# Query roots in the scale of the scores, a filled last differential head, and products between the last two norms

## The chip, the cores and the metric

The kernel runs on one NeuronCore of a Trainium2 chip. The metric is the device time of one execution in microseconds (us); lower is better. The engines named here are TensorE (PE, matrix products, its weight loads listed as PEld), VectorE (DVE), ScalarE (ACT), GpSimd (POOL) and SyncE (SP, which issues the loads).

## The reference

Two transformer blocks are computed one after the other on 512 tokens of 1024 features, in float32. The first has retention, differential attention over 8 heads, a convolution, a gated merge of the three, and a feed-forward part; then a norm. The second has a first SwiGLU part, neighbourhood attention (NA) and low-rank attention (MLA) side by side, their merge, and a second SwiGLU part. What the change touches is this:

```python
def _rmsnorm(x, g):
    y = x * lax.rsqrt(jnp.mean(x * x, axis=-1, keepdims=True) + RMS_EPS)
    return y * g

q = heads(_rmsnorm(cq, g_q) @ w_uq, N_HEADS_MLA)      # cq: 768 features of each token
s = jnp.einsum('bqhd,bkhd->bhqk', q * q.shape[-1] ** -0.5, k)
p = jax.nn.softmax(s, axis=-1)

attn = probs[:, :, 0] - lam * probs[:, :, 1]          # differential head, first block
merged = g0 * (ret @ w_branch[0]) + g1 * (diff @ w_branch[1]) + g2 * (conv @ w_branch[2])

x = x + gate * _rmsnorm(y, g_post)                    # residual of the MLA/NA merge
h = _rmsnorm(x, g_pre) * (1 + scale) + shift          # norm before the second SwiGLU
```

The root of a token's query is one factor for all 768 features of that token, and so for its whole row of scores.

## The kernel before

Activations lie with features on the partitions and tokens on the free axis, so a product takes a chunk of 128 output features by 512 tokens. Each float32 product is three products of parts rounded to fp32r: high by high, low by high, high by low. A chunk over 1024 input features is a **unit** of 24 matmuls (`unit`, L777, the matmuls at L791). Its weights pass through two buffers: SP loads `raw`, ACT copies the high part (`split`, L1444, `w_hi` at L1450), DVE subtracts for the low part (`split`, L2052, `w_lo` at L2056), and PE waits for the low part before the unit. SP may load a buffer again when the low part of the unit before is made; ACT may overwrite `w_hi` when the unit that used the buffer is done.

No scheduler orders the work. Each engine has its own program, written out in order, and semaphores tie them. Units are numbered, and the numbers fix the order of loads and splits: `U_BR` are the units of the branches' merge, `U_LORA` those of MLA's low-rank projections, `U_MLA` MLA's heads, `U_OUT2` the merged output, `U_FB` the second SwiGLU.

A head of attention leaves PE waiting for a softmax. So the kernel cuts units of the next head in parts and puts them (`fill`) between the steps of the present one. In `diff_head` (L934) the fill hangs on `more`, which is false in the last of the eight heads; that head's `qk`, `transpose_p` and `pv` steps stand alone, and `merge(1)` (L921) begins behind it with a gate unit (24 matmuls) and a branch unit.

Norms are of two kinds. A **norm over ones** (`sum_squares`, L798, the matmuls at L803) adds squares with a matrix of ones, then takes Ln and Exp on ACT (L1479, L1481), each of which loads its own function table. A **token norm** sums squares of each token into one column (`token_matmuls`, L809, 4 columns with two passes each, at L812), takes Sqrt on ACT (`token_root`, L1492), a reciprocal on DVE (`token_rooted`, L2101), and PE spreads the result over rows (`token_rows`, L830, at L775).

MLA's low-rank stage comes behind NA. PE turns NA's output (L775), runs the six `cq` units with a `sum_squares` for the keys among them, and `sum_squares` for the queries at their end. ACT copies each `cq` chunk out (L1926), splits the next weights and squares the chunk; DVE adds the squares (L2074). After the root DVE scales six chunks (L2752), ACT rounds them (`cq_hi`, L1502), DVE subtracts (`cq_lo`, L2115), and the first MLA unit takes them in turn. The unit of the rotated key part (`kr`, `U_LORA + 2`) was the fill of the last NA pair. Then the key and query parts are rotated (L1284 and L1289 on PE, L2742 to L2745 on DVE), and the first scores follow (L1324). Each score tile takes its maximum on DVE and Exp on ACT (L1957) with the constant scale 96^-0.5.

Between the merged output and the second SwiGLU stand two token norms: sums of the last chunks, root, rows, eight residual chunks on DVE (L2564, L2567), each squared on ACT (L1489) and summed on PE, then root, rows and the modulated input of the SwiGLU (L2560, L1713, L1502, L2115).

## Time and profile before

| | |
|---|---|
| three runs | 2969.21 us median (2966.67, 2969.56, 2969.21) |
| profiled execution | 2966.77 us, its span 2965.0 us |
| mean granted TensorE clock | 0.979 of full speed |
| PE busy | 2864.0 us (97% of the span) |
| DVE busy | 1486.9 us (50%) |
| ACT busy | 1163.1 us (39%) |
| DMA | 288.72 MB, mean 97 GB/s |

Times in the rows are counted from the start of the span. The granted clock is 1.00 at 2.4 GHz and 0.50 at 1.2 GHz. A busy PE can still be at the lower clock, or wait inside a group of matmuls, so the busy share alone doesn't say what a stage could give. Consecutive matmuls overlap in the rows: a pace is the distance between starts.

### The profile page before, as it was taken

What the parts mean: (1) busy time and instruction counts of PE and PEld (TensorE: products, weight loads), DVE (VectorE), ACT (ScalarE), POOL (GpSimd) and SP (SyncE); (2) the same over time, 40 slices, a digit from 0 to 9 for tenths busy, and PEclk for the clock granted to TensorE, in tenths of its full rate; (3) what the DMA queues carried; (4) which work ended last, traced back from release to release, by engine and by line L of the source; (5) the groups of instructions that cost most, each with busy time, mean ns of one, the idle gap of its engine ahead of it and who ended that gap; (6) DMA issues with size and microseconds to landing.
All of it is one profiled execution on the core that took longest, in us unless ns stands there. A gap on an engine that the chain in (4) does not pass through costs nothing.

```text
span 2965.0 us, 42739 instructions
## 1 busy us (share of the span) xinstructions
PE 2864.0 (97%) x14922; PEld 2362.3 (80%) x14922; DVE 1486.9 (50%) x2321; ACT 1163.1 (39%) x1791; POOL 34.0 (1%) x28
## 2 busy tenths in 40 slices
PE   8999999899999999999999999989989999899998
PEld 6778888679987888879998888877767778688887
DVE  3325455455565666567654473553344444433334
ACT  4323465432223322246633232355545443432223
POOL 0000000000000000000000000000000000000000
PEclk9999999899999999999999999999989999899999
DMA  3224211243343545536653333331111123133332
GB/s 114 70 65 134 79 51 56 64 139 110 119 140 103 154 144 157 163 107 193 178 142 93 92 94 97 87 84 50 49 29 48 34 54 99 54 92 93 92 92 85
DMA packets 504092, 288.72 MB, mean 97 GB/s; under 512 B 17577, under 2 KB 483962, under 8 KB 503850
## 3 DMA queue, kind: packets, MB, share of 16 engines
q1 hardware_dynamic: 503978, 287.25, 33.1%
q8 instruction: 66, 1.08, 0.2%
q14 instruction: 48, 0.39, 0.0%
HBM read 285.12 MB, written 2.10 MB: 97 GB/s over the span
## 4 chain that ended last, share of the span: by engine, by line
PE 73%; issue 19%; DVE 3%; ACT 3%; DVEq 1%; ACTq 0%; DMA 0%; POOL 0%; POOLq 0%; SPq 0%
PE unit_acc L791 65%; PE aux L775 2%; PE aux L1324 1%; PE unit_acc L1348 1%; PE unit_acc L1225 1%; DVE w_lo L2056 1%; ACT w_hi L1450 1%; PE aux L812 1%; PE aux L918 1%; PE aux L1206 1%; ACT h_hi L1502 0%; PE aux L1289 0%; ACT w_hi L1734 0%; DVE tmp L2405 0%; ACT L1496 0%
## 5 line engine op out<-in xcount | busy, mean ns | idle before, releaser
L791 PE MATMUL unit_acc<-h_hi,w_hi 128*128 128x512 f32 (+1 forms) x2376 | 829.3, 373 | 18.2 <-DVE h_lo L2115 9.4
L791 PE MATMUL unit_acc<-h_hi,w_lo 128*128 128x512 f32 (+1 forms) x2376 | 810.2, 365 | 0.0
L791 PE MATMUL unit_acc<-h_lo,w_hi 128*128 128x512 f32 (+1 forms) x2376 | 810.1, 365 | 0.0
L2056 DVE TENSOR_TENSOR w_lo<-raw,w_hi 128x1024 fp32r<-128x1024 f32 (+3 forms) x418 | 495.4, 1185 | 510.0 <-ACT w_hi L1450 503.3
L1450 ACT ACTIVATE w_hi<-raw 128x1024 fp32r<-128x1024 f32 (+3 forms) x418 | 430.5, 1030 | 699.2 <-PE unit_acc L791 655.5
L791 PEld LDWEIGHTS unit_acc<-h_hi,w_hi 128*128 128x128 f32 x2376 | 427.5, 190 | 111.7 <-issue 14.9
L791 PEld LDWEIGHTS unit_acc<-h_hi,w_lo 128*128 128x128 f32 x2376 | 426.6, 189 | 76.4
L791 PEld LDWEIGHTS unit_acc<-h_lo,w_hi 128*128 128x128 f32 x2376 | 428.1, 190 | 71.0
L791 PE MATMUL unit_acc<-branch_hi,w_hi 128*128 128x512 f32 x448 | 178.2, 398 | 0.0
L791 PE MATMUL unit_acc<-branch_hi,w_lo 128*128 128x512 f32 x448 | 177.6, 397 | 0.0
L791 PE MATMUL unit_acc<-branch_lo,w_hi 128*128 128x512 f32 x448 | 177.6, 396 | 0.0
L2229 DVE SCALAR_TENSOR_TENSOR ada_sum<-ada_raw,silu_c,ada_sum 128x512 f32<-128x512 f32 x203 | 145.8, 749 | 17.6 <-issue 12.2
L791 PE MATMUL unit_acc<-u_hi,w_hi 128*128 128x512 f32 x352 | 140.3, 398 | 0.0
L791 PE MATMUL unit_acc<-u_hi,w_lo 128*128 128x512 f32 x352 | 139.5, 396 | 0.0
L791 PE MATMUL unit_acc<-u_lo,w_hi 128*128 128x512 f32 x352 | 139.5, 396 | 0.0
L791 PE MATMUL unit_acc<-ctx_h_hi,w_hi 128*128 128x256 f32 (+1 forms) x440 | 129.0, 293 | 4.0 <-DVE w_lo L2056 2.1
L791 PE MATMUL unit_acc<-ctx_h_lo,w_hi 128*128 128x256 f32 (+1 forms) x440 | 127.0, 289 | 0.0
L791 PE MATMUL unit_acc<-ctx_h_hi,w_lo 128*128 128x256 f32 (+1 forms) x440 | 126.8, 288 | 0.0
L791 PEld LDWEIGHTS unit_acc<-branch_hi,w_lo 128*128 128x128 f32 x448 | 84.3, 188 | 20.5
L791 PEld LDWEIGHTS unit_acc<-branch_hi,w_hi 128*128 128x128 f32 x448 | 84.4, 188 | 20.4 <-DVE w_lo L2056 0.2
L791 PEld LDWEIGHTS unit_acc<-branch_lo,w_hi 128*128 128x128 f32 x448 | 84.5, 189 | 20.2
L2498 DVE TENSOR_TENSOR w_lo<-raw,w_hi 128x1024 fp32r<-128x1024 f32 (+1 forms) x66 | 78.5, 1191 | 42.9 <-ACT w_hi L1734 42.9
(367 smaller groups left out, 3610.3 us busy)
## 6 DMA issues: line engine op xcount, KB each, us to landing
raw<-in_ffn_w_dram SPq DMA_DIRECT2D x180, 512.0 KB, 3.9
raw<-in_w_in_dram SPq DMA_DIRECT2D x142, 512.0 KB, 3.9
ada_raw<-in_w_ada_dram SPq DMA_DIRECT2D x72, 512.0 KB, 4.7
raw<-in_w_up_dram SPq DMA_DIRECT2D x32, 512.0 KB, 4.2
raw<-in_w_down_dram SPq DMA_DIRECT2D x32, 512.0 KB, 3.9
raw<-in_w_branch_dram SPq DMA_DIRECT2D x24, 512.0 KB, 4.0
raw<-in_ffn_w_dram SPq DMA_DIRECT2D x24, 384.0 KB, 3.4
raw<-in_w_out_dram SPq DMA_DIRECT2D x16, 512.0 KB, 3.9
```

Of the source, the lines that this page charges most:

```text
L775: return pe.transpose(dst, src, ident[k0:k0 + k, k0:k0 + k])
L791: last = pe.matmul(G[s][0:n, 512 * j:512 * j + m], w[:, k, 0:n], x[:, k, a:a + m], start=(k == 0 and i == 0), stop=(k == kc - 1 and i == 2))
L812: done = pe.matmul(dst[:, t:t + 1], src[:, P * t:P * t + P], ones[:, 0:1], start=(first and t == 0), stop=(last and t == NT - 1))
L918: last = pe.matmul(A[1][:, a:a + 1], s[:, c * P:c * P + P], ones[:, 0:1], start=True, stop=True)
L1206: last = pe.matmul(A[0][:, 512 * e + b:512 * e + b + 256], nq[r, P * t:P * t + P], k[r, k0:k0 + 256], start=True, stop=True)
L1225: last = pe.matmul(NA_OUT[:, 64 * e:64 * e + 64], nT[:, e, j, :], nV[:, v, 64 * e:64 * e + 64], start=(e == 0 and j == 0), stop=(e == 1 an ...
L1324: last = pe.matmul(A[0][:, a:a + m], mq[0:QK, P * t:P * t + P], mk[0:QK, a:a + m], start=True, stop=True)
L1348: last = pe.matmul(MLA_OUT, mT[t % 2][:, j, :], mV[:, j, :], start=(j == 0), stop=(j == 5))
L1450: act.activation(wh[v.slot][:, 0:kc, :], raw[v.slot][:, 0:kc, :], ACT.Copy).then_inc(hi_split, 1)
L2056: dve.tensor_tensor(wl[s][:, 0:kc, :], raw[s][:, 0:kc, :], wh[s][:, 0:kc, :].bitcast(F32), ALU.subtract).then_inc(lo_split, 1)
L2229: last = dve.scalar_tensor_tensor(out=s[:, :], in0=w, scalar=c, in1=s[:, :], op0=ALU.mult, op1=ALU.add)
L2498: dve.tensor_tensor(wl[s][:, 0:kc, :], raw[s][:, 0:kc, :], wh[s][:, 0:kc, :].bitcast(F32), ALU.subtract).then_inc(lo_split, 1)
```

## The change

Five things are changed.

1. **Last differential head.** `diff_head` with `more` false takes the gate unit `U_BR[1]` in parts (`gate`): 6 matmuls behind `qk(4)`, 6 behind `qk(2)`, 3 behind `qk(1)`, 6 behind `pv(1)`, 3 behind the turn of the output. `merge(1, 1)` leaves that unit out.
2. **Root tables.** `root_table` takes a Sqrt of a constant ahead of the squares at the first block's output and at the tail of both SwiGLUs and of the second block's output. At three roots DVE's split of weights and the reciprocal change places, or ACT's.
3. **MLA query norm.** `cq` is no longer scaled. ACT squares it from PSUM and makes `cq_hi` with the gain, DVE makes `cq_lo` and adds the squares (`cq_step`, `cq_low`), token sums replace the second `sum_squares`, and the root goes, per query row, into `qsc`, which the maximum and Exp of each score tile use as scale. The `kr` unit moves from `U_LORA + 2` behind the `cq` units, so `cq` unit 0 is now the last fill of NA, and SP's loads move with it. NA's turns stand two ahead of unit 1 and two ahead of unit 2.
4. **Rotation of the key part** moves behind the first MLA unit and into the other auxiliary PSUM tile.
5. **Products between the last two norms.** `turn_over` issues 3, 4, 8, eight times 2, and 8 matmuls of 128x512 whose result nobody reads.

```diff
@@ PE
+            def merge(r, gated=0):
                 for h in range(2):
...
+                        for k in range(4):
+                            merge_pair(r, Count(U_BR[r] + 2 * k), k >= gated)
...
+                def gate(k0, k1):
+                    if not more:
+                        unit(Count(U_BR[1]), HH, HL, GM, part=(k0, k1))
...
-            pe.wait_ge(n_o, 16 + 1)
-            for c in range(4):
...
-            unit(Count(U_LORA + 3), H2H, H2L, GS)
+            pe.wait_ge(n_o, 16 + 1)
+            for half in range(2):
+                for c in range(2):
+                    na_rows(2 * half + c)
+                unit(Count(U_LORA + 3 + half), H2H, H2L, GS)
             pe.wait_ge(n_lo, 4)
             sum_squares(ss2, G2)
-            for k in range(1, 6):
-                unit(Count(U_LORA + 3 + k), H2H, H2L, GS)
-            pe.wait_ge(k_kr, 1)
-            pe.matmul(A[1][0:QK, 0:SEQ], cst("rot", 0, QK), mkr[0:QK, CTX:T2], start=True, stop=True).then_inc(k_rot, 1)
-            sum_squares(ss2, GS)
+            for k in range(3, 6):
+                unit(Count(U_LORA + 2 + k), H2H, H2L, GS)
+            unit(Count(U_LORA + 8), H2H, H2L, GS, n=QK, part=(0, 5))
+            token_sums_added(cqa, cqs, TOK[1], 6)
+            unit(Count(U_LORA + 8), H2H, H2L, GS, n=QK, part=(5, 8))
...
-            unit(Count(U_MLA), CQH, CQL, GS, kc=6, n=QK, ready=(ap_lo, 6 * KC + 2))
+            unit(Count(U_MLA), CQH, CQL, GS, kc=6, n=QK, ready=(q_lo, 0))
+            pe.wait_ge(k_kr, 1)
+            pe.matmul(A[0][0:QK, 0:SEQ], cst("rot", 0, QK), mkr[0:QK, CTX:T2], start=True, stop=True).then_inc(k_rot, 1)
...
+                for _ in range(n):
+                    pe.matmul(G[0][:, 512:1024], MH2[:, 0, 0:P], MH2[:, 0, :], start=True, stop=True)
+
+            turn_over(3)
             token_sums_added(ss2, tm2)
+            turn_over(4)
             token_rows(0)
+            turn_over(8)
             for c in range(KC):
                 token_sums(c, tm2)
+                turn_over(2)
             token_rows(1)
-            swiglu(U_FB, 6 * KC + 8, 76)
+            turn_over(8)
+            swiglu(U_FB, 6 * KC + 2, 76)
@@ ACT
+            def root_table():
+
+                act.activation(tok_std[:, NT:NT + 1], eps_col, ACT.Sqrt)
...
+                token_square(k, acc(G[v.slot], GS), cqs, SEQ)
+                act.activation(CQH[:, k, :], acc(G[v.slot], GS), ACT.Copy, scale=col_b[:, 64 + k:65 + k]).then_inc(q_hi, 1)
+                split(v + 2)
...
-                    act.activation(mP[b][:, :], A[0][:, 0:T2], ACT.Exp, bias=mst[:, b, 1:2], scale=QK ** -0.5,
+                    act.activation(mP[b][:, :], A[0][:, 0:T2], ACT.Exp, bias=mst[:, b, 1:2], scale=qsc[:, 0, t:t + 1],
@@ DVE
+                dve.scalar_tensor_tensor(out=CQL[:, k, :], in0=acc(G[s], GS), scalar=col_b[:, 64 + k:65 + k],
+                                         in1=CQH[:, k, :].bitcast(F32), op0=ALU.mult,
+                                         op1=ALU.subtract).then_inc(q_lo, 1)
+                dve.drain().then_inc(evicted[s], 1)
+                token_add(cqa[:, :], cqs, k, 6)
```

The pieces of each engine's order that the prediction rests on follow. On PE in the last differential head, from its first scores (`qk(4)`, 512 and 16 columns) on, before:

```order
L954 MATMUL aux<-diff_k_102,diff_q_100 128x512 x2
L959 MATMUL aux<-diff_k_102,diff_q_100 128x16 x2
L954 MATMUL aux<-diff_k_102,diff_q_100 128x400 x2
L775 MATMUL aux<-const,diff_vT 128x128 x4
L775 MATMUL aux<-const,diff_vT 16x128
L775 MATMUL aux<-const,diff_p_105 128x128 x4
L775 MATMUL aux<-const,diff_p_105 16x128
L954 MATMUL aux<-diff_k_102,diff_q_100 128x272 x2
L981 MATMUL aux<-diff_v,diff_pT_109 128x128 x5
```

and from `qk(2)` (272 columns) on, after:

```order
L968 MATMUL aux<-diff_k_102,diff_q_100 128x272 x2
L794 MATMUL unit_acc<-h_hi,w_hi_51 128x512
L794 MATMUL unit_acc<-h_lo,w_hi_51 128x512
L794 MATMUL unit_acc<-h_hi,w_lo_53 128x512
L794 MATMUL unit_acc<-h_hi,w_hi_51 128x512
L794 MATMUL unit_acc<-h_lo,w_hi_51 128x512
L794 MATMUL unit_acc<-h_hi,w_lo_53 128x512
L995 MATMUL aux<-diff_v,diff_pT_109 128x128 x5
```

Six matmuls of the gate unit now stand between `qk(2)` and the `pv` step that followed it at once; `gate(0, 2)` stands in the same way behind the 16-column row.

On ACT at the end of MLA's query stage, before:

```order
L1926 ACTIVATE cq<-unit_acc 128x512
L1450 ACTIVATE w_hi_52<-raw_50 128x1024
L1462 ACTIVATE tmp_1_155<-cq 128x512
L1479 ACT_TABLE_LOAD
L1479 ACTIVATE rstd_157<-aux,const 128x512
L1481 ACT_TABLE_LOAD
L1481 ACTIVATE rstd_157<-rstd_157 128x512
L1502 ACTIVATE cq_hi<-tmp_0_154 128x512
L1502 ACTIVATE cq_hi<-tmp_1_155 128x512
```

and after:

```order
L1527 ACTIVATE cq_sq_200<-unit_acc 128x512
L1912 ACTIVATE cq_hi<-unit_acc,col_b 128x512
L1488 ACTIVATE w_hi_51<-raw_49 128x1024
L1986 ACT_TABLE_LOAD
L1986 ACTIVATE tok_std<-unit_acc,const 128x4
L1989 ACTIVATE mla_kr<-unit_acc 96x512
L1488 ACTIVATE w_hi_52<-raw_50 128x1024
L1996 ACTIVATE mla_q_213<-unit_acc 96x512
```

Both roots over 512 columns and the rounding of six scaled chunks are gone; a root of 4 columns stands between the splits.

On PE between the last two norms (`ssq` and `tmp` are the sums of squares, `tok_rstd` the rows), before:

```order
L791 MATMUL unit_acc<-merged_hi,w_lo_54 128x512
L812 MATMUL aux<-const,ssq_156 128x1 x4
L812 MATMUL aux<-const,tmp_1_155 128x1 x4
L775 MATMUL aux<-const,tok_rstd 128x128 x4
L812 MATMUL aux<-const,tmp_0_154 128x1 x4
L812 MATMUL aux<-const,tmp_1_155 128x1 x4
```

and after:

```order
L1453 MATMUL unit_acc<-merged_hi 128x512 x3
L815 MATMUL aux<-const,ssq_156 128x1 x4
L815 MATMUL aux<-const,tmp_1_155 128x1 x4
L1453 MATMUL unit_acc<-merged_hi 128x512 x4
L778 MATMUL aux<-const,tok_rstd 128x128 x4
L1453 MATMUL unit_acc<-merged_hi 128x512 x8
L815 MATMUL aux<-const,tmp_0_154 128x1 x4
L1453 MATMUL unit_acc<-merged_hi 128x512 x2
L815 MATMUL aux<-const,tmp_1_155 128x1 x4
L1453 MATMUL unit_acc<-merged_hi 128x512 x2
```

The unread matmuls (L1453) stand between every two steps, the sums of each residual chunk included.

## Rows read from the trace of the kernel before

**Rows 1.** The page: busy time, share of the span and instructions of each engine.

```profile
PE 2864.0 (97%) x14922; PEld 2362.3 (80%) x14922; DVE 1486.9 (50%) x2321; ACT 1163.1 (39%) x1791; POOL 34.0 (1%) x28
```

**Rows 2.** Windows of the low-rank stage: length, PE, PEld, DVE, ACT, POOL, granted clock, DMA.

```profile
2119.04:2189.66 70.62, 52.07 (x208) 37.25 (x206) 34.97 (x46) 37.68 (x48) 0.00 (x0) 0.90 0.19 52
2125.04:2129.73 4.69, 4.69 (x22) 3.76 (x20) 2.10 (x3) 2.92 (x3) 0.00 (x0) 1.00 0.13 38
2142.40:2144.96 2.56, 2.56 (x7) 2.00 (x6) 1.18 (x2) 0.00 (x0) 0.00 (x0) 0.50 0.72 200
```

**Rows 3.** PE's timeline in the last head: start, length, instruction, [idle before <-releaser].

```profile
544.07 1.53 PE L954 MATMUL aux<-diff_k,diff_q 64*128 64x400 f32 x4 [2.68 <-DVE diff_nb L2306]
...
549.23 1.30 PE L775 MATMUL aux<-const,diff_p 128*128 128x128 f32 x5 [2.37 <-DVE diff_p L2322]
...
568.07 1.12 PE L775 MATMUL aux<-const,diff_on 128*128 128x128 f32 x4 [2.64 <-DVE diff_on L2339]
```

**Rows 4.** Busy time by stretch: the last head's slow part, and the gate unit behind it.

```profile
544.40:571.60 27.20, 20.41 (x70) 13.41 (x67) 11.76 (x37) 10.46 (x39) 1.01 (x1) 0.50 0.13 39
568.84:575.75 6.91, 6.91 (x26) 5.53 (x25) 3.05 (x5) 0.69 (x1) 0.00 (x0) 0.80 0.01 2
```

**Rows 5.** DVE's timeline at the end of that head.

```profile
569.94 0.75 DVE L2345 SCALAR_TENSOR_TENSOR branch_lo<-aux,small,branch_hi 128x512 fp32r<-128x512 f32 x1 [1.93 <-ACT branch_hi L1638]
```

**Rows 6.** Busy time by stretch: the residual chunks, and three stretches for the clock.

```profile
2547.66:2559.14 11.48, 9.25 (x44) 9.25 (x44) 10.88 (x16) 4.25 (x7) 0.00 (x0) 0.50 0.14 41
1943.76:1947.17 3.41, 1.33 (x11) 1.33 (x12) 2.96 (x4) 3.13 (x5) 0.00 (x0) 1.00 0.08 16
1947.17:1950.60 3.43, 3.43 (x18) 3.43 (x18) 2.87 (x4) 2.05 (x4) 0.00 (x0) 0.50 0.63 168
2572.90:2579.00 6.10, 3.85 (x13) 1.94 (x13) 4.77 (x7) 4.92 (x8) 0.00 (x0) 1.00 0.00 0
```

**Rows 7.** The root's table loads in the whole trace: count, ns min/median/max, first and last.

```profile
L1496 ACT ACT_TABLE_LOAD  x4: 1283/1283/1283, 951.5 to 2952.4; - x4
```

**Rows 8.** DVE's timeline, the last weight split and one scaled chunk.

```profile
2166.51 1.23 DVE L2056 TENSOR_TENSOR w_lo<-raw,w_hi 128x1024 fp32r<-128x1024 f32 x1 [3.60 <-ACT w_hi L1450]
...
2175.87 0.68 DVE L2115 TENSOR_TENSOR cq_lo<-tmp,cq_hi 128x512 fp32r<-128x512 f32 x1
```

**Rows 9.** PE's timeline in the low-rank stage, its waits.

```profile
2123.01 1.25 PE L775 MATMUL aux<-const,na_o 128*128 128x128 f32 x8 [2.94 <-DVE na_oT_lo L2722]
...
2140.36 0.50 PE L791 MATMUL unit_acc<-h_hi,w_hi 128*128 128x512 f32 x1 [3.57 <-DVE w_lo L2056]
...
2168.58 1.66 PE L803 MATMUL aux<-ssq,const 128*128 128x512 f32 x2 [3.06 <-DVE ssq L2074]
2175.26 0.71 PE L791 MATMUL unit_acc<-cq_hi,w_hi 128*96 128x512 f32 x1 [5.02 <-DVE cq_lo L2115]
...
2184.64 1.02 PE L1289 MATMUL aux<-mla_q,const 96*96 96x512 f32 x2
...
2189.66 2.07 PE L1324 MATMUL aux<-mla_k,mla_q 96*128 96x512 f32 x2 [2.50 <-DVE mla_q L2745]
```

**Rows 10.** PE's timeline between the last two norms.

```profile
2542.99 1.05 PE L812 MATMUL aux<-const,tmp 128*128 128x1 f32 x8
2546.51 1.11 PE L775 MATMUL aux<-const,tok_rstd 128*128 128x128 f32 x4 [2.46 <-DVE tok_rstd L2106]
2549.89 13.81 PE L812 MATMUL aux<-const,tmp 128*128 128x1 f32 x64 [2.27 <-ACT tmp L1489]
...
2568.52 0.77 PE L791 MATMUL unit_acc<-h_hi,w_hi 128*128 128x512 f32 x1 [3.14 <-DVE h_lo L2115]
```

**Rows 11.** ACT's timeline, the last but one query chunk.

```profile
2159.07 0.60 ACT L1926 ACTIVATE cq<-unit_acc 128x512 f32<-128x512 f32 x1 [3.11 <-PE unit_acc L791]
2159.81 1.06 ACT L1450 ACTIVATE w_hi<-raw 128x1024 fp32r<-128x1024 f32 x1
```

**Rows 12.** The Exp of MLA's 32 score tiles in the whole trace.

```profile
L1957 ACT ACTIVATE mla_p<-aux,mla_stat x32: 901/902/903, 2193.8 to 2415.1; 128x768 f32<-128x768 f32 x32
```

More of the change, by code:

```diff
@@ L401, in build @@
         CKL = at("ckv_lo", o, [2, T2], F32R); o += 8 * T2
-        cqT = at("cq", o, [6, SEQ]); o += 6 * 2048
+        cqs = [at(f"cq_sq{s}", o + s * 2048, [SEQ]) for s in range(2)]
+        cqa = at("cq_sum", o + 4096, [SEQ]); o += 6 * 2048
         CQ = o
@@ L989, in diff_head @@
                 fill(0, 0, 4)
+                gate(0, 2)
                 qk(3)
@@ L1000, in diff_head @@
                 fill(1, 0, 3)
+                gate(2, 4)
                 pv(4)
@@ L1004, in diff_head @@
                 fill(1, 3, 6)
+                gate(4, 5)
                 pv(3)
@@ L1012, in diff_head @@
                 fill(2, 2, 6)
+                gate(5, 7)
                 pe.wait_ge(d_on, val(turn(i, 1 + e, 2)))
@@ L1017, in diff_head @@
                 fill(2, 6, 8)
+                gate(7, 8)
             for k in range(3):
@@ L1187, in fill @@
                 def fill(k, k0, k1):
-                    unit(u + 3 + k, H2H, H2L, GS, n=QK if k == 2 and last_pair else P, part=(k0, k1))
+                    unit(u + 3 + k, H2H, H2L, GS, part=(k0, k1))
                 def token_v(half):
@@ L1908, in _, with na_high @@
                     na_pair(i, p, (i, p) == (1, 1))
-            for c in range(4):
+            def na_high(c):
                 act.wait_ge(n_ot, c + 1)
@@ L2723, in _ @@
                                   ALU.subtract).then_inc(n_lo, 1)
+            cq_low(0)
+            split(Count(U_LORA + 4))
+            for c in range(2):
+                na_low(c)
             for k in range(2):
                 add_square(ss2[:, :], tm2, T2, k == 0)
-            rooted()
-            scaled(2, lambda c: tm2[c % 2][:, :], lambda c: CKH[:, c, :], lambda c: CKL[:, c, :],
-                   lambda c, b: dve.scalar_tensor_tensor(out=b, in0=ckvT[:, c, :], scalar=col_b[:, 70 + c:71 + c],
-                                                         in1=rs2[:, :], op0=ALU.mult, op1=ALU.mult))
@@ L2732, in _ @@
-            for k in range(6):
-                split(Count(U_LORA + 5 + k))
-                add_square(ss2[:, 0:SEQ], tm2, SEQ, k == 0)
+            split(Count(U_LORA + 5))
+            for c in range(2, 4):
+                na_low(c)
+            cq_low(1)
+            cq_low(2)
+            split(Count(U_LORA + 6))
+            rooted()
+            for c in range(2):
+                dve.scalar_tensor_tensor(out=tm2[c][:, :], in0=ckvT[:, c, :], scalar=col_b[:, 70 + c:71 + c],
+                                         in1=rs2[:, :], op0=ALU.mult, op1=ALU.mult).then_inc(ap_tmp, 1)
@@ new lines, in _ @@
+            cq_low(3)
+            split(Count(U_LORA + 7))
+            for c in range(2):
+                nap[0] += 1
+                dve.wait_ge(ap_hi, nap[0])
+                dve.tensor_tensor(CKL[:, c, :], tm2[c][:, :], CKH[:, c, :].bitcast(F32), ALU.subtract).then_inc(ap_lo, 1)
+            for k in range(4, 6):
+                cq_low(k)
+                split(Count(U_LORA + 4 + k))
+            dve.drain()
+            dve.wait_ge(q_root, 1)
+            dve.reciprocal(tok_rstd[:, 0:NT], tok_std[:, 0:NT])
```

134 lines of the change are left out of this document (79 added, 55 removed).

## Prediction

> **What bounds the kernel now.** I read the page first: PE is busy for 97% of the span, DVE for 50%, ACT for 39% [rows 1]. So the kernel is bound by TensorE, and a change of order can give back only two things: the idle time of PE, and the stretches in which its granted clock is 0.50. I then read PE's timeline for its waits, and the windows for the clock. A matmul of 512 columns takes 4.69 / 20 = 0.2345 us warm and 2.56 / 6 = 0.427 us cold (the counts of PEld give the 20 and the 6) [rows 2]. A unit of 24 is 5.63 us warm, 10.2 cold. The reader should see that every place touched has both losses, and that they hang together: a wait is followed by a slow stretch.
>
> All sums below are against the profiled execution: 2966.8 us, a span of 2965.0 and 1.8 around it. The median of the three runs is 2.4 above that.
>
> **Last differential head.** The head waits 2.68 us for its second mask, 2.37 for its first probabilities and 2.64 for the normalised output [rows 3], and it runs at clock 0.50 from 544.4 to 571.6, with PE busy for 20.4 of 27.2 us [rows 4]. Then the gate unit takes 6.91 us, partly cold [rows 4]. The edit lays that unit's 24 matmuls into the head: 6 in the first wait, 6 ahead of `pv(4)`, 3 and 6 further on, 3 at the end. What is late next is the branch unit, which needs `branch_lo`, made at 570.69 [rows 5], against its start at 575.75, where the gate unit ends [rows 4]. With an unchanged head the gain is 575.75 - 570.69 = 5.1. The gate parts delay the head where PE was not waiting: 6 matmuls ahead of `pv(4)`, 1.4 us warm and 2.6 cold, partly taken back in later waits. Against that the head itself gets faster where the clock holds: 20.4 us busy at 0.50 would be 10.2 at full speed, though DVE and ACT own a part of the chain, so I count 6 to 7 of it. Warm throughout: 5.1 + 6.3 + nothing lost = 11.4. Cold throughout: 5.1 less 2.6 less some 1.5 for a branch unit that starts cold = 1. In the first wait 1.4 of 2.68 us is filled and the fall at 544.4 should go, but the second wait keeps 2.37 us and has no fill (the fill comes behind it). A comparable stretch, 1.33 us busy of 3.41 [rows 6], was followed by one at 0.50. So I expect one slow stretch of about 7 us around `pv(4)`, at a price of 3.4 (half its length): **-8**, bounds -1 and -11.4.
>
> **Roots with their table loaded ahead.** Four root table loads of 1.283 us are in the trace [rows 7]. The last of them, at 2952.4, stands at the kernel's end, where all that follows is on the path; it begins some way into the last sums of squares, so I count two thirds of it: **-0.9**, bounds 0 and -1.3. Behind the first SwiGLU the whole load is in the way of the rows, but DVE's split of weights (1.23 us [rows 8]), which lay beside it, now stands between root and residual. PE gets its rows and its next unit 1.2 earlier, the residual chunks start as before: **-1.2**, bounds +0.5 (if the residual sets the pace) and -2.5. At the first block's output the sums cover most of the load: **-0.25**. At the last but one norm the same exchange of split and root holds the residual where it is; its load was hidden by nothing, but see below.
>
> **MLA's query stage.** From 2119.04 to the first scores at 2189.66 are 70.6 us with PE busy for 52.1 [rows 2]. I build the new one from the same durations. NA's turns, first two: 1.04; the unit behind them, 5.63, covers the wait of 2.94 for `na_oT_lo` [rows 9]; turns 1.0; unit 5.63, which covers the making of NA's low parts; sums for the keys 1.0; three units 16.9; `kr` 5.6, cut at 5/8 by the token sums, two groups of 8 at about the 1.05 us of the row before the last norms [rows 10], 1.9; first MLA unit, 18 matmuls, 4.2 (from its start at 2175.26 to the query's rotation at 2184.64 are 9.4 [rows 9], less the second unit's 2.1 it took 7.3, since `cq_lo` came chunk by chunk; that and the 5.02 ahead of it go); rotation of the key, two wide matmuls (1.66 for such a pair while it waited [rows 9]), 1.0; second MLA unit, 12 matmuls of 384 columns, 12 x 0.2345 x 0.75 = 2.1. To here 46.0, so 2165.1 less what overlaps. Then the first scores need the rotated query. Before, from the query's rotation on PE to the scores were 5.0 us with a wait of 2.50 [rows 9]. Beside this PE chain stands a chain of DVE: rotation of the key on PE ends near 2163, then three DVE steps at the 0.68 of a 512-column step [rows 8], 2.1, two copies 1.1, two splits of 768 and 256 columns (1.23 is for 1024 [rows 8]) 1.4, three steps for the query 2.1: 2170.0. Both chains end at 2169.8 to 2170.1. **-19.8**.
>
> What can go less well: the wait of 3.57 for `w_lo` [rows 9] came when DVE and ACT had the keys' root between the splits. That work still stands there, and each `cq` round is now longer: on ACT a square and a copy from PSUM (0.60 each [rows 11]) ahead of the 1.06 of `w_hi` [rows 11]; on DVE `cq_lo` and the sum (0.7 each) ahead of the 1.23 of `w_lo` [rows 8]. With hand-overs this is 4.3 us from the end of a unit to the weights of the next but one, against 5.63 that PE has for the unit between. The tight round is `cq` unit 5, 0.2 us to spare by my sum. If that wait comes back at its old 3.57 and brings its cold stretch of 3.4 us (price 1.7), the gain is 19.8 - 5.3 = 14.5; I keep 13 as the low bound and 21 as the high one (the 0.50 stretch avoided and the key's rotation earlier).
>
> **Scales by pointer.** Exp has 768 columns in 0.902 us with one pointer operand [rows 12]; copies have 0.60 for 512 and 1.06 for 1024 [rows 11], so 0.83 for 768. A pointer then costs up to 0.07, 32 times: 2.3 at most if all of it is on the path, nothing at the least, since PE's fills lie beside most tiles. I take **+0.5**. On DVE the maximum's scale is in the same case.
>
> **Products between the last two norms.** Before, PE waits 2.46 for the rows, 2.27 for the first square, then runs 64 one-column matmuls in 13.81 us (1.73 per chunk), at clock 0.50 [rows 6, 10]. DVE's eight chunks take 11.48 us, 1.44 each [rows 6]: less than PE's 1.73. So this stretch is set by a cold PE. The residual starts no earlier: the 3 + 4 products and the moved split (1.23) take what the hidden table load gives. Then each chunk costs PE its 8 sums and 2 products. If the clock stays at 0.50: 1.73 + 2 x 0.427 = 2.58 per chunk, 0.85 more; over the seven chunks ahead of the last sums 6.0, and 0.3 more since the last pair delays the rows: **+6.3**. If it holds at 1.00: 8 sums at 0.95 or so and 0.47, about DVE's 1.44, so DVE sets the pace: 8 x (1.73 - 1.44) = 2.3 and a little at the rows, -2.6. The 8 products behind the rows fall in the wait of 3.14 for `h_lo` [rows 10] and cost nothing warm, 0.3 cold. Which it is I read from the windows. The sums alone kept PE busy for 9.25 of 11.48 us and the clock was 0.50 [rows 6]: busy by one-column matmuls does not raise it. With the products, full-width work is 0.47 of 1.44 us, a third. 1.33 of 3.41 (39%) was followed by 0.50, 3.85 of 6.10 (63%) stayed at 1.00 [rows 6]. A third lies on the side of the fall. The page "TensorE: Matmul & The Clock Gate" of the Trainium skill, section "HAM oscillation — how this bites in real kernels", gives as the abstract rule that PE must have no long idle gaps, and by it the clock would hold, since the longest gap left is under 1.5 us. The rows speak against it here, as the stretch of sums had small gaps too and stayed slow; the rule's outcome is the first rival.
>
> Sum: 2966.8 - 8 - 0.9 - 1.2 - 0.25 - 19.8 + 0.5 + 6.3 = 2943.4; on the median of the shown runs 2945.8. Forecast **2945**, its own range 2939 to 2951.
>
> **Rivals.**
> - *The clock holds between the last norms.* The products fill every gap, and 8 of them stand ahead of the first sums. For it: the stretch begins warm behind a full unit. Against it: the shares above. Its term is -2.6 in place of +6.3: 2936.
> - *The head stays cold, or the `cq` rounds slip.* For it: the wait of 2.37 is unfilled and 6 cold matmuls then delay `pv(4)`; the margin of 0.2 at `cq` unit 5. Against it: full-width matmuls in four places of the head. With -1 for the head 2952; with 13 for MLA's stage 2952 as well; both 2959.
> - *Slower: PE waits in every `cq` round.* ACT reads each chunk twice from PSUM and DVE once, ahead of the next split. If the round takes longer than 5.63, PE waits seven times, and if each wait is followed by the low clock, as that of 3.57 was, all seven units run at 10.2: 7 x 4.6 = 32 us more than planned, 2945 + 32 = 2977. It decides from a round of some 6.5 us on, 2.2 more than my 4.3; against it also that a cold unit gives the others time, so that the next wait would go.
> - *It does nothing*, the gains of MLA's stage being eaten by the tail behind it: against it, the six scaled chunks are on the path as their own five waits show, and they are gone.
>
> **How the numbers follow.** Forecast 0.62, clock holds 0.20, cold head or slipped rounds 0.14, slower 0.03, nothing 0.01. The range runs from 2933 (the first rival with the head warm) to 2956 (the second, short of both together). A measurement of this kernel can tell about 0.2%, 5.9 us, from no change. The first three cases lie all but wholly below 2963: faster 0.95; same 0.02; slower 0.03.
>
> **What would show it.** In the changed kernel's profile: the last head with a branch unit starting 8 us nearer to `qk(4)` and one slow stretch; the first MLA scores some 50.8 us behind NA's last fill, no wait over 1 us in the six units, no wait ahead of the first MLA unit; the token sums between the last norms at 2.6 us per chunk and clock 0.50 (1.4 and 1.00 would be the rival); the Exp at 0.90 to 1.0 us. The forecast is wrong if the stretch between the last norms is shorter than before, if the head is still cold throughout, or if the `cq` units wait for `w_lo`.

## The result, and the profile after

The changed kernel takes 2945.55 us (median of four runs, 2942.68 to 2947.37) against 2967.94 before (four runs, 2961.93 to 2969.56), a ratio of 0.9927 with a 95% interval of 0.991 to 0.9945. Faster, by 22 us; 2945 was predicted. The profiled execution took 2945.81 with a span of 2944.0, against 2966.77 and 2965.0. The page of after (busy time and instructions; the chain that ended last, which on the page before was PE 73%, issue 19%):

```profile
PE 2866.4 (97%) x14975; PEld 2368.9 (80%) x14975; DVE 1482.9 (50%) x2317; ACT 1159.8 (39%) x1787; POOL 33.9 (1%) x28
...
PE 82%; issue 8%; DVE 5%; ACT 3%; DVEq 1%; ACTq 0%; DMA 0%; POOL 0%; POOLq 0%; SPq 0%
```

PE is as busy as before. The chain's shares say little about the gain: "issue", time in which an engine waited for nothing that the profile shows, fell by 11 points of the span, some 330 us by the two pages, for a gain of 21. So the reading goes by stretches. Since all marks of the program can be found in both traces, the 21.0 us of difference between the spans can be laid out by stretch. Each row is the distance between the starts of two instructions on PE (the last: on DVE):

| stretch | before | after | difference | predicted |
|---|---|---|---|---|
| start to `qk(4)` of the last head | 540.13 | 540.95 | +0.8 | 0 |
| to the first branch unit behind it | 35.62 | 28.38 | -7.2 | -8 |
| to the rows of the first block's norm | 377.59 | 377.31 | -0.3 | -0.25 |
| to the sums at the first SwiGLU's tail | 953.55 | 953.66 | +0.1 | 0 |
| to the rows there | 3.66 | 2.41 | -1.25 | -1.2 |
| to the first unit on the latent tokens | 48.92 | 50.42 | +1.5 | 0 |
| to NA's turns | 159.57 | 159.52 | 0 | 0 |
| to MLA's first scores | 70.62 | 50.67 | -19.95 | -19.8 |
| to MLA's turns (eight heads) | 233.98 | 234.78 | +0.8 | +0.5 |
| to the end of the last output unit | 118.50 | 118.37 | -0.1 | 0 |
| to the turn of x, behind the first unit of the second SwiGLU | 43.28 | 48.87 | +5.6 | +6.3 |
| to the sums at the end | 365.01 | 364.99 | 0 | 0 |
| to the output on DVE | 3.87 | 3.04 | -0.8 | -0.9 |

**The last head.** PE's timeline, the rows that answer to [rows 3], and the branch unit:

```profile
544.88 0.94 PE L968 MATMUL aux<-diff_k,diff_q 64*128 64x400 f32 x4 [1.08 <-DVE diff_nb L2366]
...
549.45 1.30 PE L778 MATMUL aux<-const,diff_p 128*128 128x128 f32 x5 [2.93 <-DVE diff_p L2382]
...
554.61 1.62 PE L995 MATMUL aux<-diff_v,diff_pT 128*128 128x128 f32 x10
...
569.33 0.39 PE L794 MATMUL unit_acc<-branch_hi,w_hi 128*128 128x512 f32 x1
```

The first wait is 1.08 us instead of 2.68, the third is gone, the second has grown from 2.37 to 2.93. `pv(4)` starts at 554.61, 5.2 behind the turn of the probabilities (2.4 before). The clock in that stretch, and in a fast one and a slow one behind it:

```profile
549.45:554.61 5.16, 5.16 (x15) 3.46 (x16) 3.04 (x10) 1.87 (x6) 0.00 (x0) 0.50 0.54 165
555.00:561.00 6.00, 4.79 (x32) 3.45 (x30) 2.81 (x13) 3.15 (x14) 0.00 (x0) 1.00 0.03 13
562.00:568.00 6.00, 5.49 (x15) 3.43 (x15) 0.86 (x2) 1.50 (x8) 1.01 (x1) 0.50 0.01 3
```

So the head has two slow stretches, 548.1 to 554.9 and 561.8 to 568.6, instead of one of 27 us.

**The low-rank stage.** Its window, and PE's rows that answer to [rows 9]:

```profile
2112.65:2163.32 50.67, 47.23 (x221) 36.66 (x219) 30.11 (x42) 30.81 (x40) 0.00 (x0) 0.99 0.23 64
```

```profile
2151.16 0.39 PE L794 MATMUL unit_acc<-cq_hi,w_hi 128*96 128x512 f32 x1
...
2155.35 1.02 PE L1424 MATMUL aux<-mla_kr,const 96*96 96x512 f32 x2
...
2163.32 2.08 PE L1348 MATMUL aux<-mla_k,mla_q 96*128 96x512 f32 x2 [2.50 <-DVE mla_q L2838]
```

PE waits for 3.4 of 50.7 us, all of it behind the second MLA unit, and the clock is 1.00 up to there. None of the waits of 2.94, 3.57, 3.06 and 5.02 us is left.

**Between the last two norms.** PE and then DVE, the rows that answer to [rows 10]:

```profile
2519.88 0.60 PE L778 MATMUL aux<-const,tok_rstd 128*128 128x128 f32 x4
...
2523.97 1.48 PE L815 MATMUL aux<-const,tmp 128*128 128x1 f32 x8 [1.64 <-ACT tmp L1527]
2525.31 1.20 PE L1453 MATMUL unit_acc<-merged_hi 128*128 128x512 f32 x2
2526.31 1.70 PE L815 MATMUL aux<-const,tmp 128*128 128x1 f32 x8
2527.87 1.20 PE L1453 MATMUL unit_acc<-merged_hi 128*128 128x512 f32 x2
...
2544.23 1.05 PE L778 MATMUL aux<-const,tok_rstd 128*128 128x128 f32 x4
```

```profile
2520.60 1.23 DVE L2116 TENSOR_TENSOR w_lo<-raw,w_hi 128x1024 fp32r<-128x1024 f32 x1 [1.08 <-ACT w_hi L1488]
2521.75 0.74 DVE L2624 SCALAR_TENSOR_TENSOR y<-y,res_gain,aux 128x512 f32<-128x512 f32 x1
```

The rows are there at 2519.88, but DVE first waits for `w_hi`, splits, and starts the residual at 2521.75; PE then waits 1.64 us for the first square. During the first chunk the clock falls, and from then on each chunk costs 2.56 us: eight sums at 1.56 and two products together at 1.00 (2526.31, 2527.87). DVE's residual was done by 2533.2, eleven us before PE.

**The root at the first SwiGLU's tail.** DVE before and after, and the ACT Exp of all MLA tiles, which answers to [rows 12]:

```profile
1908.69 1.23 DVE L2056 TENSOR_TENSOR w_lo<-raw,w_hi 128x1024 fp32r<-128x1024 f32 x1 [2.04 <-ACT w_hi L1450]
1910.32 0.18 DVE L2106 RECIPROCAL tok_rstd<-tok_std 128x4 f32<-128x4 f32 x1 [0.40 <-ACT tok_std L1496]
1911.71 0.75 DVE L2564 SCALAR_TENSOR_TENSOR y<-y,res_gain,aux 128x512 f32<-128x512 f32 x1 [1.21 <-PE aux L775]
```

```profile
1902.47 0.18 DVE L2166 RECIPROCAL tok_rstd<-tok_std 128x4 f32<-128x4 f32 x1 [2.44 <-ACT tok_std L1538]
1904.20 1.22 DVE L2116 TENSOR_TENSOR w_lo<-raw,w_hi 128x1024 fp32r<-128x1024 f32 x1 [1.55 <-ACT w_hi L1488]
1905.35 0.74 DVE L2624 SCALAR_TENSOR_TENSOR y<-y,res_gain,aux 128x512 f32<-128x512 f32 x1
```

```profile
L2015 ACT ACTIVATE mla_p<-aux,mla_stat,mla_scale x32: 991/992/994, 2167.6 to 2389.6; 128x768 f32<-128x768 f32 x32
```

From the sums (1906.89 before, 1900.30 after) the reciprocal comes at 3.43 before and 2.17 after, the residual at 4.82 and 5.05: the split now stands between.

### The profile page after: what moved, and what is told of

It reads as the page before. It is cut to its first block, busy times and chain, and to the rows that moved or that the text cites. A ratio compares the mean times of both kernels' runs of the same rounds, so it can differ in the third digit from the quotient of the medians.

```text
span 2944.0 us, 42823 instructions
## 1 busy us (share of the span) xinstructions
PE 2866.4 (97%) x14975; PEld 2368.9 (80%) x14975; DVE 1482.9 (50%) x2317; ACT 1159.8 (39%) x1787; POOL 33.9 (1%) x28
## 4 chain that ended last, share of the span: by engine, by line
PE 82%; issue 8%; DVE 5%; ACT 3%; DVEq 1%; ACTq 0%; DMA 0%; POOL 0%; POOLq 0%; SPq 0%
PE unit_acc L794 71%; PE aux L778 3%; PE unit_acc L1372 1%; PE aux L1348 1%; DVE w_lo L2116 1%; PE aux L995 1%; PE unit_acc L1244 1%; PE aux L968 1%; ACT w_hi L1488 1%; PE aux L815 1%; PE aux L921 1%; PE aux L1225 1%; DVE diff_p L2356 0%; PE unit_acc L1453 0%; ACT mla_p L2015 0%
```

## The experiments

Small differences are read in their own stretch of the trace, because the same instructions elsewhere vary by more (last section). These are the stretches on which the readings rest, in us, from the profiled execution of each:

```
                     qk(4) to   SwiGLU 1   rows to   NA turns    MLA's     last output
                     branch     sums to    first     to first    eight     unit to
                     unit       rows       unit      scores      heads     turn of x
before               35.62      3.66       48.92     70.62       233.98    43.28
after                28.38      2.41       50.42     50.67       234.78    48.87
e1_no_turn           28.69      2.41       50.62     50.67       233.51    42.52
e2_mla_only          34.46      3.67       48.14     50.67       233.56    43.28
e3_turn_only         35.64      3.67       50.82     71.69       234.03    44.73
e4_head_only         28.40      3.66       49.06     70.43       232.55    43.29
e5_head_wait         27.69      2.41       51.95     50.67       233.53    47.95
e6_late_split        28.48      2.41       50.31     50.67       234.81    43.88
e7_turn_six          28.58      2.41       51.97     50.67       234.94    48.04
e8_combined          27.71      2.41       50.45     50.67       234.81    40.93
e9_turn_eight        27.69      2.41       51.72     50.67       233.57    40.53
e10_rotate_first     27.23      2.41       51.95     49.08       233.75    40.91
e11_const_scale      28.59      2.41       50.42     50.67       233.51    48.02
e12_turns_together   28.42      2.41       51.85     56.88       233.49    46.37
```

### One part of the change at a time

e1_no_turn takes the unread products out of the changed kernel:

```diff
-            turn_over(3)
             token_sums_added(ss2, tm2)
-            turn_over(4)
             token_rows(0)
-            turn_over(8)
             for c in range(KC):
                 token_sums(c, tm2)
-                turn_over(2)
             token_rows(1)
-            turn_over(8)
```

> The changed kernel without the 39 unread products between the last two norms. Theory (the products lengthen a stretch that stays at clock 0.50): 5.6 us less than the changed kernel, about 2940, ratio to the kernel before 0.9905; token sums back at 1.73 us per chunk, clock 0.50 there. Rival (the products pay for themselves, by keeping the clock up in front of the second SwiGLU): the same time as the changed kernel or more, 2945 to 2949.

Measured: 2940.34 us (2936.42 to 2942.94), ratio 0.9909 (0.9894 to 0.9925). The stretch is 42.52 instead of 48.87, 6.35 less. The products cost a little more than was said (5.6); the rival falls. The median moved by 5.2; in the profiled execution other stretches, of the same instructions, happened to be longer by 3.1, 1.5 and 1.1.

e2_mla_only is the changed kernel with all but the MLA part taken back:

```diff
-                    if not more:
+                    if False:
                         unit(Count(U_BR[1]), HH, HL, GM, part=(k0, k1))
-            merge(1, 1)
+            merge(1)
-            root_table()
-            turn_over(3)
...
```

> The kernel before with the new query norm of MLA alone (with the moved key unit, the moved turns of NA and the scales by pointer); no gate unit in the last head, no root tables, no unread products. Theory (terms are independent): 19.9 less in the low-rank stage and 0.7 more for the scales, 19.3 less in all, ratio 0.9935. Rival (a part of the 20 us comes from the phase in which the stage starts, and would be smaller without the filled head): 10 to 15 less, ratio 0.995 to 0.9965.

Measured: 2945.86 (2943.4 to 2948.13), ratio 0.993 (0.9917 to 0.9944), 20 us. The low-rank stage is 50.67, to the hundredth that of the changed kernel. The gain doesn't depend on where the stage begins.

e3_turn_only adds the products alone to the kernel before:

```diff
+            turn_over(3)
             token_sums_added(ss2, tm2)
+            turn_over(4)
             token_rows(0)
+            turn_over(8)
             for c in range(KC):
                 token_sums(c, tm2)
+                turn_over(2)
             token_rows(1)
+            turn_over(8)
```

> The kernel before with the 39 unread products alone. The table load (1.28 us) is not hidden here, so the gaps are wider. Theory: slower by 5.5 to 6.5 us, ratio 1.002, clock 0.50 in the sums. Rival (the products hold the clock at 1.00 in this place): faster by 2 to 3 us, ratio 0.999.

Measured: 2967.68 (2963.83 to 2971.54, eleven runs), ratio 1.0007 (0.9998 to 1.0016). Neither number came: the stretch is 1.45 us longer than before, not 5.5. PE's timeline of this kernel:

```profile
2548.54 0.65 PE L775 MATMUL aux<-const,tok_rstd 128*128 128x128 f32 x4 [0.80 <-DVE tok_rstd L2116]
...
2551.45 1.05 PE L812 MATMUL aux<-const,tmp 128*128 128x1 f32 x8 [0.41 <-ACT tmp L1499]
...
2552.92 1.01 PE L812 MATMUL aux<-const,tmp 128*128 128x1 f32 x8
...
2557.55 1.70 PE L812 MATMUL aux<-const,tmp 128*128 128x1 f32 x8
```

Here the wait ahead of the first sums is 0.41 us. The first three chunks run at clock 1.00, 1.43 to 1.46 us each, the fourth takes 1.77; only then comes the slow pace of 2.56. In this kernel DVE's split still lies ahead of the reciprocal, so the residual starts 0.7 behind the rows, not 1.9.

e4_head_only adds the gate unit's parts alone:

```diff
+                gate(0, 2)
...
+                gate(2, 4)
                 pv(4)
...
-            merge(1)
+            merge(1, 1)
```

> The kernel before with the gate unit laid into the last differential head alone. Theory: the branch unit starts 28.4 us behind qk(4) instead of 35.6, 7.2 less in all, ratio 0.9976. Rival (the gain is given back by the merge behind it, whose weights come later): under 3 less, ratio 0.999 to 1.

Measured: 2956.36 (2950.96 to 2957.31), ratio 0.9964 (0.995 to 0.9977). The stretch is 28.40, and the merge behind it is as long as before (377.57 to the norm's rows, 377.59 before): nothing is given back. The median is 9.4 below that of before, more than the 7.2 of the stretch; the rest is not traced to anything.

### Why the products didn't hold the clock

e6_late_split moves DVE's split of weights behind the residual chunks; the products stay:

```diff
             token_rooted()
-            split(Count(U_OUT2 + 1 + KC))
             residual(1, ROW[0])
+            split(Count(U_OUT2 + 1 + KC))
```

> The changed kernel with DVE's split of weights between the last two norms moved behind the eight residual chunks; the unread products stay. It shortens the wait of 1.64 us ahead of the first sums to about 0.4. From the end of the last output unit to the turn of x: 43.28 us before the change, 48.87 after it, 44.73 with the products alone on the kernel before. Theory (the longer wait lets the clock fall at the first chunk instead of the fifth): 43 to 44, five to six us less than the changed kernel, the first four chunks at 1.4 us and clock 1.00. Rival (the share of full-width work alone decides, the wait does not): the start comes 1.25 earlier and all chunks stay at 2.6, 47.6.

Measured: 2942.88 (2936.25 to 2943.93), ratio 0.9922 (0.9909 to 0.9936); the stretch is 43.88, in the theory's range. PE's timeline:

```profile
2522.68 1.05 PE L815 MATMUL aux<-const,tmp 128*128 128x1 f32 x8 [0.41 <-ACT tmp L1527]
...
2524.14 1.02 PE L815 MATMUL aux<-const,tmp 128*128 128x1 f32 x8
...
2528.93 1.70 PE L815 MATMUL aux<-const,tmp 128*128 128x1 f32 x8
```

With a wait of 0.41 instead of 1.64 us the clock is 1.00 for three chunks (1.46, 1.43 and 1.42 us) and a part of the fourth (1.95), then it falls as well. In the changed kernel it falls in the first.

That the wait makes this difference is not shown. e5_head_wait, e11_const_scale and e12_turns_together below have the same instructions in this stretch as the changed kernel, and the same wait of 1.64, but the stretch takes 47.95, 48.02 and 46.37 us instead of 48.87. In the first two the slow pace comes with the second chunk, in e12_turns_together with the third:

```profile
2528.64 1.05 PE L815 MATMUL aux<-const,tmp 128*128 128x1 f32 x8 [1.64 <-ACT tmp L1527]
...
2530.11 1.02 PE L815 MATMUL aux<-const,tmp 128*128 128x1 f32 x8
...
2531.54 1.21 PE L815 MATMUL aux<-const,tmp 128*128 128x1 f32 x8
```

So behind one and the same wait the fall comes 0.5 to 3.6 us behind the start of the first sums (four traces); with a wait of 0.41 it comes 5.1 and 5.3 us behind it (e6_late_split, e3_turn_only). That speaks for the theory. But counted from the end of the last output unit the clock falls at 11.1 us in e12_turns_together and at 11.4 in e6_late_split, nearly at the same time with either wait. One trace of each doesn't part the wait from the scatter. What the earlier split gives for certain is the earlier start of the sums, 1.2 to 1.3 us.

e7_turn_six has six products behind each chunk:

```diff
                 token_sums(c, tm2)
-                turn_over(2)
+                turn_over(6)
```

> The changed kernel with six unread products behind each chunk's sums instead of two. Theory (more full-width work holds the clock, 1.41 of 2.4 us): clock 1.00 through all eight chunks at 2.4 us each, 19 us for them, about what they take with two (20.5). Rival (the clock is low in this place whatever PE does): 1.73 + 2.56 = 4.3 us a chunk, 14 us slower.

Measured: 48.04 for the stretch, where the changed kernel has 48.87, and clock 1.00 from the second chunk on:

```profile
2521.71 1.27 PE L815 MATMUL aux<-const,tmp 128*128 128x1 f32 x8 [1.62 <-ACT tmp L1527]
2522.84 2.91 PE L1453 MATMUL unit_acc<-merged_hi 128*128 128x512 f32 x6
...
2527.95 0.95 PE L815 MATMUL aux<-const,tmp 128*128 128x1 f32 x8
2528.76 1.65 PE L1453 MATMUL unit_acc<-merged_hi 128*128 128x512 f32 x6
```

```profile
2528.80:2541.61 12.81, 12.81 (x78) 11.22 (x79) 2.22 (x4) 2.80 (x5) 3.52 (x1) 1.00 0.00 0
```

The clock in this place follows what PE does. But a chunk takes 2.3 us (the first 3.8, since its six products ran slow), more than 1.73 at the low clock without products: holding the clock costs more than it gives, when the work that it speeds up are one-column sums.

### Where the head's time is

e5_head_wait puts nine of the gate unit's matmuls where PE waits longest:

```diff
+                gate(2, 5)
                 transpose_p(4)
                 qk(2)
-                gate(2, 4)
                 pv(4)
                 transpose_p(3)
                 qk(1)
-                gate(4, 5)
```

> The changed kernel with nine of the gate unit's matmuls laid into the wait for the first probabilities (2.93 us, empty so far), in place of the six behind qk(2) and the three behind qk(1). Theory (that empty wait makes the clock fall for 6.7 us, and the six matmuls delay the first pv): clock 1.00 from qk(4) to pv(4), the branch unit 25 us behind qk(4) instead of 28.4, 3.4 us less in all than the changed kernel. Rival (the softmax chain of DVE and ACT sets the head's length): 27.5 to 28.4, under 1 us less.

Measured: 2946.61 (2944.49 to 2946.84), ratio 0.9937 (0.9924 to 0.9951). The head is 27.69, 0.7 shorter, in the rival's range. Its timeline and its clock:

```profile
544.26 0.50 PE L794 MATMUL unit_acc<-h_hi,w_hi 128*128 128x512 f32 x1 [0.83 <-ACT diff_v L1661]
...
546.46 0.71 PE L778 MATMUL aux<-const,diff_p 128*128 128x128 f32 x5
...
548.00 1.57 PE L995 MATMUL aux<-diff_v,diff_pT 128*128 128x128 f32 x10 [0.17 <-ACT diff_pT L1644]
550.90 0.66 PE L778 MATMUL aux<-const,diff_p 128*128 128x128 f32 x4 [1.33 <-DVE diff_p L2381]
```

```profile
541.79:552.28 10.49, 7.87 (x45) 5.17 (x45) 6.53 (x20) 6.64 (x21) 0.00 (x0) 1.00 0.30 100
552.28:565.55 13.27, 11.98 (x36) 8.40 (x37) 4.09 (x16) 4.15 (x18) 1.01 (x1) 0.51 0.01 1
```

The first slow stretch is gone, as the theory said, and `pv(4)` starts 10.1 behind `qk(4)` instead of 13.7. But PE then waits 1.33 us for the next probabilities, and the second slow stretch begins at once and lasts to the end of the head: 13 us instead of 6.8. Of 3.5 us won, 2.8 went there.

### Versions that might beat both

e8_combined is e1_no_turn with the edits of e5_head_wait and e6_late_split.

> The changed kernel without the unread products, with the nine gate matmuls in the empty wait of the last head and with DVE's split behind the residual chunks. Theory: 5.6 + 0.8 less from the products (as in the run without them), 3.4 from the head, 1.25 from the split: ratio to the kernel before 0.989, about 2934. Rival (a gain ahead of a stage is given back by the clock in the next): no better than the run without products alone, 0.991.

Measured: 2939.41 (2935.15 to 2942.32), ratio 0.9917 (0.9903 to 0.993). In its stretches: 27.71 for the head, and 40.93 between the norms, 1.59 less than e1_no_turn (1.25 was expected). As a whole it fell short of what was expected, and its interval overlaps that of e1_no_turn, so the times alone don't tell them apart.

e9_turn_eight puts eight products back behind the first rows of e8_combined:

```diff
             token_rows(0)
+            turn_over(8)
             for c in range(KC):
                 token_sums(c, tm2)
```

> The combined kernel with eight unread products put back in one place only, behind the first rows, where PE waits 2.27 us for the first square. From the end of the last output unit to the turn of x it is 40.93 us in the combined kernel. Theory (a filled wait lets the clock fall later, as with the late split, and nothing is added between the sums): the first two or three chunks at 1.43 instead of 1.73, 40.0 to 40.3. Rival (eight products only move the fall by their own length, the sums start later behind them): 40.9 to 41.5.

Measured: 2938.24 (2935.17 to 2940.76), ratio 0.9913 (0.9896 to 0.9929); the stretch 40.53. Between the two. PE shows why:

```profile
2518.70 1.12 PE L778 MATMUL aux<-const,tok_rstd 128*128 128x128 f32 x4 [0.57 <-DVE tok_rstd L2161]
2519.47 3.22 PE L1452 MATMUL unit_acc<-merged_hi 128*128 128x512 f32 x8
2522.53 2.04 PE L815 MATMUL aux<-const,tmp 128*128 128x1 f32 x16
2524.94 10.12 PE L815 MATMUL aux<-const,tmp 128*128 128x1 f32 x48 [0.37 <-ACT tmp L1522]
```

The clock had already fallen while PE waited 0.57 for the rows (1.12 us for them instead of 0.65), the products ran slow (3.22 us for eight), and the clock came back to 1.00 for two chunks and into the third.

e10_rotate_first, on e8_combined, changes two places:

```diff
+            mla_ready(0, 0, 0)
             for k in range(2):
                 split(Count(U_MLA + 2 + k), 2 if k else 6)
-            mla_ready(0, 0, 0)
...
-                gate(2, 5)
+                gate(2, 4)
                 transpose_p(4)
                 qk(2)
                 pv(4)
+                gate(4, 5)
                 transpose_p(3)
```

> The combined kernel with two changes that are read in their own stretches. (1) DVE rotates the first query ahead of the two splits of weights. Theory (the chain rotation of the key, copies, splits, rotation of the query is what the first scores wait for): from NA's turns to the first scores 49.1 instead of 50.67. Rival (PE's own chain is as long, as the prediction's sum had it): 50.3 to 50.7. (2) In the last head the gate unit's three matmuls that stood in the wait for the first probabilities stand behind the first pv, in a wait of 1.33: theory (a low clock behind the first pv sets the rest) 26.5 to 27 us from qk(4) to the branch unit instead of 27.7; rival (chain of DVE and ACT) 27.7. Together about 2 us less than the combined kernel if both theories hold.

Measured: 2935.32 (2932.94 to 2935.54), ratio 0.99 (0.9883 to 0.9916), the lowest median of the study, though its interval overlaps those of e8 and e9. From NA's turns to the first scores it takes 49.08:

```profile
2158.60 1.02 PE L1313 MATMUL aux<-mla_q,const 96*96 96x512 f32 x2
...
2162.03 1.56 PE L1348 MATMUL aux<-mla_k,mla_q 96*128 96x512 f32 x4 [0.91 <-DVE mla_q L2833]
```

The wait ahead of the scores is 0.91 instead of 2.50: the DVE chain was the end of that stage, 1.6 us behind PE's own. The head is 27.23, between theory and rival.

### Two sizes inside MLA

e11_const_scale leaves the query's root out of the scores:

```diff
-                    act.activation(mP[b][:, :], A[0][:, 0:T2], ACT.Exp, bias=mst[:, b, 1:2], scale=qsc[:, 0, t:t + 1],
+                    act.activation(mP[b][:, :], A[0][:, 0:T2], ACT.Exp, bias=mst[:, b, 1:2], scale=QK ** -0.5,
...
-                    dve.tensor_scalar(mst[:, b, 1:2], mst[:, b, 0:1], qsc[:, 1, t:t + 1], None, ALU.mult).then_inc(k_log, 1)
+                    dve.tensor_scalar(mst[:, b, 1:2], mst[:, b, 0:1], -(QK ** -0.5), None, ALU.mult).then_inc(k_log, 1)
```

> The changed kernel with the constant scale back in the Exp and the maximum of MLA's score tiles; the query's root is left out of the scores. From the first scores to MLA's turns it is 234.78 us in the changed kernel and 233.98 before. Theory (the pointer costs 0.09 us per tile and is on the path in some tiles): 234.0 to 234.3. Rival (the difference is the clock's, 0.2 to 0.8 in such a stretch from run to run): no different from 234.8 beyond that.

Measured: 233.51 for the eight heads, a little below what the theory gave. It decides little, since the ten kernels with the pointer have 233.49 to 234.94 (mean 234.1) and the four without 232.55 to 234.03 (mean 233.5). The Exp takes 902 ns here and 992 with the pointer, 32 x 0.09 = 2.9 in all. The means differ by 0.6, which is within the scatter, so no share of the 2.9 is shown to be on the path.

e12_turns_together undoes one detail of the order:

```diff
-            for half in range(2):
-                for c in range(2):
-                    na_rows(2 * half + c)
-                unit(Count(U_LORA + 3 + half), H2H, H2L, GS)
+            for c in range(4):
+                na_rows(c)
+            for half in range(2):
+                unit(Count(U_LORA + 3 + half), H2H, H2L, GS)
```

> The changed kernel with the four turns of NA's output together again, ahead of query unit 1, instead of two ahead of unit 1 and two ahead of unit 2. From NA's turns to the first scores it is 50.67 us in the changed kernel and 70.62 before. Theory (the unit between the turns hides the making of NA's low parts, a wait of 2.9 us before): 53.5 to 54, with a wait of about 3 for na_oT_lo. Rival (the rounds of DVE and ACT behind it take the wait up, since PE then asks later for each weight): 51 to 52.

Measured: 56.88, 6.2 more than the changed kernel, twice what the theory gave. PE, and then a window over most of the unit behind:

```profile
2117.20 1.97 PE L778 MATMUL aux<-const,na_o 128*128 128x128 f32 x8 [3.53 <-DVE na_oT_lo L2793]
```

```profile
2118.83:2125.60 6.77, 6.77 (x24) 5.42 (x23) 0.62 (x1) 0.00 (x0) 0.00 (x0) 0.72 0.16 47
```

The wait is 3.53. Nearly all of the other 2.7, which the theory left out, are matmuls at the low clock behind it: the last two turns take 0.8 more than in the changed kernel, and the two units behind them 1.6 more. This is a single run, but the stretch takes 50.67 in all nine traces that have the changed kernel's instructions there. So some 6 of the 20 us of this stage come from two turns put elsewhere.

## Why the prediction was right, point by point

**The head, -8 forecast, -7.2 measured** (e4_head_only alone: -7.2). The step was to expect the first wait filled, the second empty, and one slow stretch of 7 us around `pv(4)`. That stretch is there, 548.1 to 554.9, just ahead of `pv(4)`. A second one of 6.8 us at the end was not foreseen. Priced like the first, at half its length, it would cost 3.4, but the forecast missed by only 0.8; so another part of the head's sum was too cautious by some 2.6 (an estimate from these two numbers), and that the number came so close is in part luck. That the rest of the head's length is DVE's and ACT's was put in as "6 to 7 of 10.2", and e5_head_wait showed how little is left to win there by PE's order.

**Root tables: right in the parts, wrong in one sum.** At the end -0.8 (0.9 forecast). At the first block's output the rows start 3.73 us behind the first sums before (949.61 to 953.34) and 3.50 after (943.14 to 946.64), -0.23 against the -0.25 forecast. At the first SwiGLU's tail PE did get its rows 1.25 earlier, and the prediction took that as the gain, since PE "gets its next unit 1.2 earlier". But the residual on DVE started 0.2 later, the units and sums behind depend on it, and the stretch behind the rows was 1.5 longer: the 1.25 by which the rows come earlier and the 0.2. The step that failed is the one that read the gain at PE though DVE sets the pace there; the text had that as its bound of +0.5, and the sum of both rows is +0.25. The table load's time was real, and the exchange of split and root spent it. No run tried the order alone. From the sums to the first unit behind, both columns of the table together, the four kernels with the old order have 51.8 to 54.5 us and the ten with the new one 52.7 to 54.4. So the gain of 1.2 is not there, and a loss isn't shown either.

**The low-rank stage, -19.8 forecast, -19.95 measured**, the same in e2_mla_only. The sum from durations held because all waits in it were found: PE's chain and DVE's chain were built apart, and the later one was taken. The prediction thought them equal; e10_rotate_first shows that DVE's was later by 1.6. The feared slip at `cq` unit 5 didn't come.

**The scales, +0.5 forecast**: +0.8 in the profiled pair, and not told from the scatter. The price of a pointer was put at up to 0.07 us; it is 0.09, so the upper bound of 2.3 should have been 2.9.

**Between the last norms, +6.3 forecast, +5.6 measured**, and e1_no_turn has 6.35 less than the changed kernel. The forecast chose the low clock by likeness to the stretches in [rows 6], and the rival failed: behind the wait of 1.64 us PE had no gap at all, and from the first chunk on the clock was 0.50. The page "TensorE: Matmul & The Clock Gate" of the Trainium skill, section "HAM oscillation — how this bites in real kernels", gives as its abstract rule only that PE must have no long idle gaps. This trace doesn't agree: the one gap in the sums' way was 1.64 us (the prediction had said under 1.5), and the clock fell. What the forecast lacked is that the fall can come later than the first chunk. It took the low clock for all eight chunks; in the four traces with these same instructions the stretch is 3.1, 4.7, 4.7 and 5.6 us longer than before, as the slow pace begins with the third, the second or the first chunk. The measured 5.6 is the worst of the four, and so the closeness to 6.3 is in part luck. With a wait of 0.41 ahead of them the products cost 1.45 (e3_turn_only against before) and 2.95 (e6_late_split against e8_combined), with 1.64 they cost 3.85 to 6.35 (against e1_no_turn). Whether the wait makes this difference is open, as said above.

That the forecast hit the median within 1 us is luck in part. For the profiled execution the sum gave 2943.4, and 2945.81 was measured. This miss of 2.4 is +0.8 ahead of the head, +0.8 in it, +1.5 behind the first tail and +0.3 for the scales, against -0.7 between the norms and small ones. The forecast then added 2.4 for the distance from the profiled execution to the median, as before had it; in the changed kernel that distance is -0.3.

## What to carry to other kernels

Price a wait of TensorE as the wait plus the slow matmuls behind it: in e12_turns_together 3.5 became 6.2. Where a norm's factor is constant over a row of scores, put it in the scale of the scores; what it saves is the chain of scaling and rounding ahead of the next product, 20 us here with the reordering. Before filling a gap with work that nobody reads, look for who makes the gap: moving one DVE instruction behind the residual gave 1.6 us, while the 39 products cost 1.5 to 6.4. And before a fall of the clock is put down to one cause, look at other traces of the same instructions: here it moved by 3 us among four of them.

## What the runs showed of the hardware

- One-column matmuls keep PE busy, but not its clock. In the changed kernel PE is busy without a gap from 2523.97 to 2544.23, about two fifths of it with products of 512 columns (1.00 of 2.56 us in each chunk), and the granted clock is 0.51:

```profile
2523.97:2544.23 20.26, 20.26 (x80) 18.57 (x81) 8.97 (x14) 4.68 (x8) 3.51 (x1) 0.51 0.06 17
```

- Six products per chunk instead of two raise the same place to 1.00 (e7_turn_six).
- Identical instruction streams differ from run to run by single slow stretches. From the first branch unit to the norm's rows the kernels with the filled head have 376.4 to 380.4 us, from the first unit on the latent tokens to NA's turns 158.0 to 161.1. That is 3 to 4 us per stretch, more than several edits of this study are worth, and the reason why these were read in their own stretches. The stretch between the last two norms does it too: 46.4 to 48.9 us in four traces.
- An Exp of 768 columns with a second pointer operand takes 0.992 instead of 0.902 us.
